# Projection stage: the rotation angles of a tile are requested one tile earlier on SyncE's queue

## The reference, cut to what matters

```
z = h @ w_in                       # h: 2064 tokens x 1024
q_a, kv_a, k_pe, q_g, k_g, v_g = split(z)
q  = rmsnorm(q_a) @ w_q_b          # per head 128 plain + 64 rotated columns
kv = rmsnorm(kv_a) @ w_kv_b        # per head 128 key + 128 value columns
k_rot = rotate(k_pe, cos, sin)
qg = axial(rmsnorm(q_g)); kg = axial(rmsnorm(k_g)); vg = v_g
```

## Time and profile before

| | |
|---|---|
| median of 3 runs | 5683.69 us (5683.55 to 5691.12) |
| profiled execution, device time | 5683.11 us |
| its span in the profile | 5682.0 us |
| PE busy over the span | 5347.5 us, 94% |
| DVE busy over the span | 3611.7 us, 64% |
| granted clock of PE, mean | 0.974 |
| projection stage | about 1033 to 1476 us from the start of the span |

### The profile page before, as it was taken

The page is one execution under the profiler, slowest core; times in us unless marked ns, Lnnn a source line. Parts: engine busy times, 40 slices in busy tenths (PEclk is TensorE's granted clock), DMA queues, the critical chain, the costliest instruction groups (busy, mean ns, idle before and its releaser), DMA issues. The chain is left out here.

```text
span 5682.0 us, 92418 instructions
## 1 busy us (share of the span) xinstructions
PE 5347.5 (94%) x30192; PEld 4768.3 (84%) x30193; DVE 3611.7 (64%) x6799; ACT 2641.7 (46%) x5250; POOL 828.4 (15%) x611
## 2 busy tenths in 40 slices
PE   8999979789799999998878999999999999999993
PEld 7777768678699999997767999999899888889893
DVE  6667757433466667776774745655667745577777
ACT  3444321333455556665333633543556534366664
POOL 1101125323100000000450100100101101011113
PEclk9999989899899999999989999999999999999997
DMA  3332234344511011201423744644557735477676
GB/s 143 115 115 101 93 126 166 121 136 131 166 60 49 25 44 42 93 10 56 149 97 123 239 146 156 202 170 151 188 196 232 242 118 169 145 223 257 240 232 230
DMA packets 260437, 809.25 MB, mean 142 GB/s; under 512 B 22304, under 2 KB 168448, under 8 KB 224512
## 3 DMA queue, kind: packets, MB, share of 16 engines
q1 hardware_dynamic: 230352, 717.05, 36.2%
q0 software_dynamic: 27536, 84.88, 6.7%
q10 hardware_dynamic: 2336, 4.45, 0.2%
HBM read 662.84 MB, written 143.47 MB: 142 GB/s over the span
## 5 line engine op out<-in xcount | busy, mean ns | idle before, releaser
L2723 DVE TENSOR_TENSOR e_wl<-r_raw,e_wh 128x1024 fp32r<-128x1024 f32 x770 | 930.7, 1223 | 438.8 <-DVEq L2351 435.3
L2572 PE MATMUL ps<-e_hT,e_wl 128*128 128x192 f32 (+5 forms) x4096 | 1196.1, 292 | 0.0
L2639 ACT CAST e_wh<-r_raw 128x1024 fp32r (+1 forms) x770 | 790.8, 1043 | 860.4 <-ACTq L2351 848.1
L2565 PE MATMUL ps<-e_hT,e_wh 128*128 128x384 f32 (+2 forms) x2560 | 795.7, 374 | 5.3 <-PEq L2351 4.0
L2572 PEld LDWEIGHTS ps<-e_hT,e_wl 128*128 128x128 f32 x4096 | 776.1, 189 | 10.6
L2567 PE MATMUL ps<-e_hT,e_wh 128*128 128x352 f32 (+2 forms) x1536 | 529.0, 344 | 7.3 <-PEq L2351 7.3
L2571 PE MATMUL ps<-e_hT,e_wh 128*128 128x352 f32 (+2 forms) x1536 | 527.0, 343 | 0.0
L2565 PEld LDWEIGHTS ps<-e_hT,e_wh 128*128 128x128 f32 x2560 | 480.3, 188 | 48.4 <-issue 7.7
L2593 PE MATMUL ps<-e_wh,e_aTh 128*128 128x512 f32 x1248 | 504.4, 404 | 4.9 <-PEq L2351 4.8
L1746 PE MATMUL ps<-a_PT,a_V 128*128 128x256 f32 (+1 forms) x3264 | 504.3, 294 | 0.2 <-DVE a_PT L1831 0.2
L1791 ACT CAST a_PT<-ps 128x512 fp32r<-128x512 f32 x512 | 288.0, 589 | 464.7 <-PE ps L1731 464.7
(11 more groups left out here) (370 smaller groups left out, 9613.0 us busy)
## 6 DMA issues: line engine op xcount, KB each, us to landing
r_raw<-in_wgu SPq DMA_DIRECT2D x130, 2048.0 KB
r_raw<-in_wdn SPq DMA_DIRECT2D x64, 2048.0 KB
m_raw<-in_w SPq DMA_DIRECT2D x56, 1024.0 KB, 4.8
qTd<-p_qt SPq DMA_DIRECT2D x32, 640.0 KB, 6.6
e_bd<-in_bdn SPq DMA_DIRECT2D x32, 512.0 KB, 3.8
kTd<-p_kt SPq DMA_DIRECT2D x32, 448.0 KB, 4.0
a_Q<-qTd SPq DMA_DIRECT2D x7, 2048.0 KB, 9.6
a_V<-vd SPq DMA_DIRECT2D x24, 512.0 KB, 4.5
```

The costliest lines, as they stand in the source:

```text
L2565: t = pe.matmul(both, wh, E.hT[:, :, k, 0:v], start=(k == 0), stop=False)
L2572: t = pe.matmul(p[:, 0:v], wl, E.hT[:, 0, k, 0:v], start=False, stop=(k == 7))
L2639: act.copy(E.wh[:, h, x], raw[:, 2048 * h + 1024 * i:2048 * h + 1024 * i + 1024]).then_inc(E.hi_full, 1)
L2723: return dve.tensor_tensor(lo, src, hi.bitcast(F32), ALU.subtract)
```

## The change

Tile n + 1's angles are requested at the point of the loop where tile n's were. Tile 0's are requested just before tile 1's. The waits for the buffer move along with the request: at the head of tile n, SyncE now waits for "yg" and "rot" of tile n - 1.

```diff
+    def angles(n):
+        if n >= NT:
+            return
+        if n >= 2:
+            sp.wait_ge(*P.g.at("yg", n - 2))
+            sp.wait_ge(*P.v.at("rot", n - 2))
+        sp.dma_start(P.rp[:, n % 2], A["rope"][P.tiles[n][1]]).then_inc(*P.rpld[n % 2].more())
+
     load(0)
     load(1)
     for n, t, r, whole in P.tiles:
-        if n >= 2:
-            sp.wait_ge(*P.g.at("yg", n - 2))
-            sp.wait_ge(*P.v.at("rot", n - 2))
         if n == 0:
             sp.wait_ge(*P.v.at("w2", 3))
-        sp.dma_start(P.rp[:, n % 2], A["rope"][t]).then_inc(*P.rpld[n % 2].more())
+            angles(0)
+        angles(n + 1)
         for k in range(2, 5) if n == 0 else (n + 4,):
             load(k)
         if n == NT - 1:
```

## The result

The changed kernel takes 5649.55 us (median of 5 runs, 5647.59 to 5655.15) against 5683.69 us before (5 runs, 5680.14 to 5691.12). The ratio is 0.9939 with a 95% interval of 0.9924 to 0.9953: 34 us, or 0.6%, faster. The forecast was 5651 us, within a range of 5644 to 5661. The profiled execution has a span of 5646.6 us against 5682.0.

The account below looks back on a forecast made before the run. TensorE, busy 349.49 of 388 us in the steady stretch, was taken as the bound, so only its idle or lower-clock time could be won: 22.6 + 6.6 + 2.8 = 32.0 us, 5683.1 - 32.0 = 5651.1 us, range 5644 to 5661.

Parts of the forecast that it names:

- The waits: Projection stage: VectorE's waits for the angles, in 15 of 17 tiles, all go; ScalarE's 0.9 us stands in their place.
- Term 1: TensorE's 13 waits at the value product L1261 for VectorE's low half go whole: 22.6 us, bounds 19 and 22.6.
- Term 2: TensorE's time at 1.2 GHz after waits in tiles 2, 4, 5 and 12 goes: 6.6 us, bounds 0 and 6.6.
- Tile 7: TensorE's 3.87 us wait at L1251 stays; the later lower clock counts 0, with 2 us at the upper end.
- Term 3: End of the projection stage, tile 16: 2.8 us won, limited by full transfers; bounds 0 and 6.6.
- The sum: All gains together, 22.6 + 6.6 + 2.8 = 32.0 us, off the profiled 5683.1 us.
- clock passages stay: Rival: TensorE's four stretches at the lower clock, 1.65 us each, have another cause and remain; 5657.7 us, chance 0.18.
- The wait changes hands: Rival: ScalarE's high half holds VectorE, L1261 starts as late; 5680 us; chance 0.07 including only part won.
- Slower, by the tighter buffer wait: Rival: SyncE's buffer wait at the tile's head delays value stores and ScalarE; 5694.5 us or more, chance 0.03.
- A wait of SyncE for GpSimd: Sign that would show the prediction wrong; the buffer wait was claimed always met, with 8.3 us of cover in tile 1.

Follow-up runs that it names:

- mid_tile: Changed kernel with tile n + 1's angles requested within tile n, between its key stores and query stores; 5651.04 us.
- turn_first: Kernel before, with VectorE making the low halves of the next input ahead of its wait for the angles; 5677.69 us.
- some_early: Changed kernel with angles requested a tile sooner only for tiles 2, 4, 5, 7 and 12, the others at the old place; 5670.29 us.
- later: Kernel before, with the 512 KB input of tile n + 4 requested ahead of the angles; 5710.05 us.
- last_late: Changed kernel with tile 16's angles alone requested at the old place; 5654.12 us.
- keys_early: Changed kernel with 3.4 MB of the attention's rotated and plain keys loaded one tile sooner; 5649.91 us (6 runs), then 5648.74 us (5 runs).

## Why the prediction was right

**The waits.** As forecast: 15 waits of VectorE for the angles gone, ScalarE's 0.85 us in their place.

**Term 1, 22.6 us.** Measured 22.4; 0.2 us is left, in tile 8. What was named as late next, ScalarE's high half, is late next, and costs nothing, by little: in tile 1 the first low half ends near 1085.1 and the key product at 1085.25. `mid_tile` shows how much room there is (the rotation may wait 1.4 to 1.7 us for its angles), and `turn_first` where it ends: with the rotation 1.6 us after the key product, GpSimd's chain binds. That second limit was not in the prediction.

**Term 2, 6.6 us.** Measured 6.6: tiles 2, 4, 5 and 12 are at 23.1 us with a granted clock of 1.00. The step rested on the order of events in four tiles. It is shown now: take the waits of these tiles away and the passages go (`some_early`), take them away without touching the transfers and they go too (`turn_first`), lengthen the waits and they come in eight tiles and tile 7 (`later`). The argument for it in the prediction, that no passage comes without a wait of 1.4 us or more, is too strict: 0.92 us with 0.47 us shortly ahead brought one. The page of the Trainium skill that I set against it, "TensorE: Matmul & The Clock Gate", Part 1, ties the 1.2 GHz state to idleness; as I read it strictly, 6.6 us would have stayed. I read it too strictly: the same part also tells of a kernel whose short idle times between groups of matmuls made the clock go down and up again, and the trace here agrees, with a granted clock of 0.50 for some 2 us behind a wait of 1.42 us (1110 to 1112 us in the kernel before) and 1.00 soon after. Waits of 0.9 to 3.6 us inside a busy stretch were enough, though not every one.

**Tile 7.** I put the rest of its lower clock at 0 with 2 us at the upper end. Measured: the tile went from 31.47 to 24.68 us, 6.8 less, of which 5.2 are the wait. So 1.6 us, nearly the upper end. This is the term most mis-sized, and the rows say why. The kernel before had two passages in this tile and not one, the second of them behind the 5.17 us:

```profile
1229.80:1232.00 2.20, 2.17 (x11) 2.20 (x12) 0.00 (x0) 1.26 (x4) 0.00 (x0) 0.50 1.04 283
1232.00:1236.00 4.00, 1.49 (x10) 1.30 (x9) 0.16 (x2) 1.35 (x3) 0.00 (x0) 0.92 0.97 288
1236.00:1240.00 4.00, 1.34 (x6) 1.34 (x7) 3.73 (x11) 0.00 (x0) 1.91 (x2) 0.51 0.04 12
```

The granted clock (third number from the end) is 0.50, then 0.92, then 0.51: it had come back before the long wait and fell again. The second passage is one more of the kind of term 2, and counted at 1.65 us like the other four it would have brought the sum to some 33.7. The first one, behind the 3.87 us, is what is left in the changed kernel. In the other traces in which tile 7's angles are early and VectorE's order is the usual one the tile takes 24.2 to 25.1 us, and 25.6 in `some_early`, so this part varies.

**Term 3, 2.8 us.** Measured 3.1, by itself in `last_late`. The reason held too: the engines are done 6.2 us sooner, but the transfers let only 3.1 through, and with fewer transfers at this place another 2.5 come. How the 3.1 split into free transfer time (2.1 in the prediction) and angles no longer asked for (0.7) was not measured.

**The sum.** In the stage 32.0 us were forecast and 34.2 came: 1.6 from tile 7, 0.3 from the end, 0.3 in tile 6. The two differences outside it, 1.7 us ahead and 2.9 behind, are not counted as the change's. Ahead of tile 0, 0.75 us is older than the stage, and 0.97 is the clock, which came back later after the meeting (0.51 against 0.64 granted from 1024 to 1034 us). Over all 14 traces it takes 36.0 to 36.2 us from that meeting to tile 0's transposes in nine and 36.8 to 37.0 in five, and either group holds kernels that ask for tile 1's angles at the start (`last_late`; the changed one) and kernels that don't (the one before; `mid_tile`). Behind the stage, two traces of the kernel before give 4206.0 and 4207.1 us, two of the changed one 4203.1 and 4206.6, and all 14 traces lie between 4203.1 and 4216.2. So that the median came within 1.5 us of the forecast is partly luck: what lies behind this stage varies by 13 us between traces, more than any term but the first.

**The range.** It does not separate the forecast from its main rival: "clock passages stay" gives 5657.7, inside 5644 to 5661. The tiles decide between them, not the time. The upper end also counts term 2 with 4 us, where the prediction's own lower bound for it is 0; with 0 it would be 5664.

**The rivals.** "Clock passages stay" is out by `some_early`, `turn_first` and `later`. "The wait changes hands" is out for this change; `turn_first` shows a near relative of it, 5677.7 us, where L1261 waits no longer and L1287 does. "Slower, by the tighter buffer wait" is out too, and the step it rests on, that this wait is always met, held everywhere. One line of the changed kernel's view of SyncE's waits, 1238 to 1250 us, seems to say otherwise:

```profile
SPq L1164 <- POOL w2r L1496: 1.7, 1, 1.7
```

A wait of SyncE for GpSimd was one of the signs that would have shown the prediction wrong. The timeline shows that it is none:

```profile
1225.19 1.85 POOL L1502 TENSOR_TENSOR w2r<-w2r 128x768 f32<-128x768 f32 x1
...
1233.01 2.88 SPq L1191 DMA_DIRECT2D qTd<-p_qt  x2
...
1235.99 2.40 SPq L1164 DMA_DIRECT2D w2r<-in_rope  x1
...
1236.50 1.15 POOL L1496 TENSOR_TENSOR w2r<-w2r 16x64 f32<-16x64 f32 x4
```

The request at 1235.99, for tile 9's angles, waits for the end of GpSimd's last pass (L1502) in tile 7, and that had come at 1227.04. It follows the query stores by 0.1 us and takes the 2.40 us that it takes in most tiles. L1496 is a pass of tile 8 that happens to end within those 2.40 us. The next request, for tile 10, comes behind the key stores of tile 8, at 1252.21, and tile 8's last pass ended at 1239.26. What a wait there would cost was not tried.

## What to carry to other kernels

A small table that is asked for behind large stores on the same queue arrives late, and the engine that waits for it need not be the one that loses: follow the wait to the next product that needs that engine's later work. Price the wait there, add what the clock may lose behind each wait, and check the step for all who wait for it, since moving the waiting step instead of the request mostly moved the wait (`turn_first`). Where a list of waits contradicts the program, look at the timeline before believing it: of the waits read here, some were put down to the wrong engine and one was not there at all. At a stage's end, look at the transfers before counting what the engines gain.

## What the runs showed of the hardware

Three things I had not expected. A wait of TensorE as short as 0.92 us, with one of 0.47 us shortly ahead of it, was followed by a passage at 1.2 GHz (`some_early`, tile 6), while waits of 1.57 and 1.64 us in the kernel before were not, and neither was one of 2.67 us in `later`; and yet two traces of the same kernel have the passages in the same four tiles, so it looks like a matter of timing more than of chance from run to run. What decides which short wait brings a passage stays open. Second, a request of 512 KB set ahead of the angles made TensorE's waits only 1.1 to 1.7 us longer in most tiles (`later`). The stores ahead on the queue matter more: from request to landing the angles took 6.5 us (median) behind the query stores, 4.5 us ahead of them (`mid_tile`), and 2.4 to 2.6 us at the least. Third, SyncE took longer to issue its requests while the transfers were full: the same three took SyncE 1.84 us while the transfers' busy share was 0.51 (`keys_early`, tile 16), and 4.84 us (the kernel before) and 7.42 us (the changed one) while it was 1.00 and 1.01.
